# Compressed key scores of a decode step from weighted queries, and unread products in idle stretches

## The chip, the cores and the metric

One core of one Trainium2 chip runs one program, a single launch. The metric is the device time of one execution in microseconds, the median of several runs.

## The reference

One layer of a hybrid decoder is applied to a prompt of 1024 tokens and to 8 decode sequences of 4 new tokens each over a cache of 2048 tokens. All data are fp32. One input projection feeds two head groups: NSA (8 heads in 2 groups, with compressed, selected and window branches) and MLA (4 heads on latent rows). Their outputs are gated, joined, projected, added to the input and normalised.

What matters here is the compressed branch of a decode sequence. A compressed key is formed for every pair of neighbouring 16-token chunks of the cache, and scores are its products with the queries:

```python
def compress(k, w, pe):
    ...
    ch = k[:, :n_chunks * CMP_STRIDE].reshape(B, n_chunks, CMP_STRIDE, G_A, HD_A)
    blk = jnp.concatenate([ch[:, :-1], ch[:, 1:]], axis=2) + pe[None, None, :, None, :]
    return jnp.einsum('bnlgd,lde->bnge', blk, w)

    s = jnp.einsum('btgrd,bngd->btgrn', q, kc).astype(jnp.float32) * scale
```

`w` is 32 token positions by 64 by 64. A sequence has 128 chunks and 127 compressed keys, 2 groups, and 16 query rows (4 tokens by 4 heads) in a group, so 32 rows in all.

## The kernel before

The kernel is written by hand for each engine: the order of the calls is the order in which an engine works, and semaphores with counted values are the only waits. Five stages follow one another: the input projection (0 to 384 us), its preparation and the prompt's attention (to 798), the output projection of 8 prompt tiles (798 to 918), decode of 8 sequences (918 to 1153), and the output projection of the decode rows (to the end).

**Head.** `pe_projection` (L414) multiplies the conditioning rows with w_ada (L427), waits for the sums (`s_us`, `s_modD`), transposes them (L442), waits for the modulation on VectorE (`s_modt`), transposes the first prompt tile's tokens (L554) and starts the decode rows' first projection (L456) when its weights have come.

**Output projection.** In `pe_out` (L1669) a tile m is 8 transposes of the next tile (L1676) and two times 8 calls of 128x128 weights on 512 columns (L1695). In tiles 5 to 7 `chunk` (L1919) adds the first sequence's page transposes between them. VectorE and ScalarE evict and normalise. On SP's queue `sp_out` (L1642) loads what decode needs: biases at m = 1, queries and the compression weights (`load_compressors`, L1969) at m = 2, pages of sequence 0 at m = 3 and 4, its latents and window at 5 and 6.

**Decode.** `pe_decode_loop` (L2060) runs one iteration for each sequence b. TensorE first compresses keys: `compress(b, 0, 0, 16)` is 16 token positions by 2 groups, 32 calls at L2079 with weights of 64 rows by 128 columns (the two halves of the 32 positions side by side) on the 128 chunks. The result stands in banks 3 and 4; ScalarE copies it to RBK with the position bias added (L2259). Window scores (L2090) stand between, then the compressed scores (L2100): 4 calls of a query block `QC`, built by POOL for each sequence, against RBK, shifted by one chunk for the second half. Then come latent scores (L2114), the transposes of the probabilities (L2134 to L2136, which wait on `s_cv` for VectorE's PG, L2366), the value compression (L2079 again, 64 records more), importance, selected scores, the value products (L2153 to L2177), and between them the page transposes of the next sequence (L1925), which VectorE and ScalarE copy to `XT`.

VectorE's order in an iteration: the copy of the former sequence's output (L2341), the turn of the selected keys (L2332), the window scores' subtraction (L2348), the compressed softmax to PG (L2359 to L2366), the copy PTI (L2375), and later the ranking, the other softmaxes, and at the end the turns of window (L2325) and latents (L2309) for the next sequence.

POOL builds `QC`, then the window and selected query blocks `QB` (L2497), then `QM` (L2501); `built(b, n)` is the count that TensorE waits for. Before the first of these it finishes the last tile's norm, which waits for ScalarE's square of that tile (L1760). SP loads 16 pages of 256 KB for a sequence once the buffer is free (L2013), its window (L2024) and 16 latent blocks (L2018). At the end of the last iteration there are no page transposes; TensorE multiplies with FM (L2217, L2224), waits for VectorE's last turn PTS (L2434), forms the selected values (L2175, L2177), two small products (L2231, L2234) and the rows' output projection (L1713), behind which VectorE waits for gate rows loaded in 32 small transfers.

Of the kernel before, what the change touches and what calls it, by code (L numbers as in the profile page):

```python
# [20 lines left out]
P = 128  # L21
# [95 lines left out]
def build(nc, x_prompt, x_sample, cache_nsa, cache_mla, state_win, page_table, c_prompt, c_sample,  # L117
# [3 lines left out]
    with ExitStack() as ctx:  # L121
# [14 lines left out]
        ql_dram = nc.dram_tensor("sample_q_latent", (P, P), F32, kind="Internal").ap()  # L136
        qr_dram = nc.dram_tensor("sample_q_rope", (64, P), F32, kind="Internal").ap()
# [275 lines left out]

        def pe_projection(pe):  # L414
# [5 lines left out]
            for k in range(KT):  # L420
# [10 lines left out]
                if k == 1:  # L431
# [6 lines left out]
                    pe.transpose(PS[:, 0, 128:138], GST[0:10, :], ident[0:10, 0:10]).then_inc(s_u, 1)  # L438
            pe.wait_ge(s_us, 1)
# [3 lines left out]
            mm.then_inc(s_mt, 1)  # L443
            pe.wait_ge(s_modt, 2)
# [1187 lines left out]
        def sp_out_loads(sp):  # L1632
# [7 lines left out]
            sp.dma_start(GF, g_final.rearrange("(o n) -> o n", o=1).to_broadcast([P, DM])).then_inc(s_gp, 16)  # L1640

        def sp_out(sp, tiles, at):  # L1642
            for m, j in enumerate(tiles, at):
# [25 lines left out]
        def pe_out(pe, tiles, at):  # L1669

            def transposes(m, j):
                if m >= 1:
                    pe.wait_ge(s_yTA, m)
                    pe.wait_ge(s_yTD, m)
                for f in range(8):
                    mm = pe.transpose(PS[:, f // 4, P * (f % 4):P * (f % 4) + P], Z[:, j - 1, P * f:P * f + P], ident)  # L1676
# [5 lines left out]
            for m, j in enumerate(tiles, at):  # L1682
# [10 lines left out]
                for c in range(2):  # L1693
# [3 lines left out]
                    mm.then_inc(s_po, 1)  # L1697
                    if m >= 5:
# [48 lines left out]
        def act_out(act, tiles, at):  # L1747
            copy = lambda o, i: act.activation(o, i, ACT.Copy)
            for m, j in enumerate(tiles, at):
# [3 lines left out]
                if m + 1 < at + len(tiles):  # L1753
                    out_copies(act, copy, 0, s_yTA, m + 1)
                if m >= 5:
# [4 lines left out]
                act.activation(JK[0:n, :], YO[m % 2][0:n, :], ACT.Square, accum_out=SSO[0:n, m:m + 1]).then_inc(s_so, 1)  # L1760

# [4 lines left out]
        def dve_out(dve, tiles, at):  # L1766
            for m, j in enumerate(tiles, at):
# [11 lines left out]
                for c in range(2):  # L1779
# [6 lines left out]
                        .then_inc(s_g2, 1)  # L1786
                if m < NT - 1:
# [35 lines left out]
        IMS, IMJ, RK, MK = dsm(30), dsm(15), dsm(15), dsm(16)  # L1823
        G1, G2 = dsm(450), dsm(450)
        DMN, MN, SUM, NMX, RCD = dsm(12), dsm(4), dsm(4), dsm(4), dsm(4)
        QC = [dsm(128).rearrange("p (g s q) -> p g s q", g=G, s=2) for _ in range(2)]
# [10 lines left out]
        WC2 = view(33152, 4096).rearrange("p (k l m) -> p k l m", k=2, l=16)  # L1837
        KT4 = view(42400, 2048).rearrange("p (j c) -> p j c", j=4)
# [24 lines left out]
        RING = [(0, n) for n in CHUNK_ITEMS[0] + CHUNK_ITEMS[1]]  # L1863
# [9 lines left out]
        BY_ACT = {it: it[1] in (("K0", "K2", "K3", "V0", "V2") if it[0] else ("K0", "K2", "V0", "V2")) for it in RING}  # L1873
# [15 lines left out]
        def bank_of(b, name):  # L1889

            m = AT[b, name]
            if m < FRONT:
                return PS[:, 0 if name == "V3" else 6 + m % 2, :]
# [11 lines left out]
        def next_bank(pe, b, name):  # L1905

            m = AT[b, name]
            if m < FRONT:
                if 2 <= m and name != "V3":
# [17 lines left out]


# [22 lines left out]
        def load_queries(sp):  # L1951
# [8 lines left out]
            for s in range(2):  # L1960
                sp.dma_start(QSREP[64 * s:64 * s + 64, :, :, :].rearrange("p g b q -> p g (b q)"),
                             qs_dram.rearrange("(g d) x -> d g x", g=G)).then_inc(s_nb, 16)
            sp.wait_ge(s_qd, 8)
# [5 lines left out]
        def load_compressors(sp):  # L1969
            for k, w in enumerate((w_cmp_k, w_cmp_v)):  # L1970
                for g in range(G):
                    for s in range(2):
                        sp.dma_start(WC2[64 * g:64 * g + 64, k, :, 64 * s:64 * s + 64],
                                     w[0, 16 * s:16 * s + 16].rearrange("l d e -> d l e")).then_inc(s_nb, 16)
# [7 lines left out]
        def load_mask(sp):  # L1982
            sp.wait_ge(s_qd, 9)
# [4 lines left out]
        def load_late(sp):  # L1988
            sp.wait_ge(s_late, 64)
            sp.wait_ge(s_qd, 10)  # L1990
# [9 lines left out]
        NB_EARLY = 16 * (24 + 14 + 3 + 8 + 1)  # L2000
# [26 lines left out]
        def store_window(sp, b):  # L2027
            sp.wait_ge(s_wn[b % 2], 16 * (b // 2) + 16)
# [4 lines left out]
        def sp_decode(sp):  # L2033
            load_mask(sp)
            for b in range(1, NB):
# [8 lines left out]
                load_window(sp, b)  # L2044
                load_latent(sp, b, pages)
# [536 lines left out]
```

## Time and profile before

| | us |
|---|---|
| median of 3 runs | 1170.86 (1169.98 to 1173.89) |
| profiled execution | 1170.58 |
| its span, first to last instruction | 1168.8 |
| TensorE busy (matmul) | 1125.3 |
| VectorE busy | 547.6 |
| ScalarE busy | 350.5 |
| POOL busy | 86.5 |

The mean granted TensorE clock is 0.983 of full speed. The page gives busy time for each engine; an fp32 matmul call appears as two records on TensorE, a transpose as one, and both have a weight load (PEld) each. A mean duration of a record is its latency and is longer than the distance between two, since records overlap: the busy time of a group over its count is the better price. The granted clock is 1.00 at 2.4 GHz and 0.50 at 1.2 GHz.

### The profile page before, as it was taken

To read this page: it belongs to the slowest core of one execution; us is meant where nothing else is said; L and a number is where in the kernel's file an instruction comes from. 1 tells how busy PE (TensorE), PEld (TensorE's weight loads), DVE (VectorE), ACT (ScalarE), POOL (GpSimd) and SP (SyncE) were. 2 spreads that over 40 slices of the span, in tenths; PEclk is the share of its full clock that TensorE was granted. 3 is DMA by queue.
4 is the path that set the end of the run, shared out by engine and by line. 5 is a ranking of instruction groups with operands and counts; after the bars stand their busy time and mean duration, and the time that the engine had idled before them with its cause. 6 is when DMAs were issued, how large, how long until landed. Compare 5 with 4: busy or idle time off the path is not lost.

```text
span 1168.8 us, 21316 instructions
## 1 busy us (share of the span) xinstructions
PE 1125.3 (96%) x7918; PEld 739.6 (63%) x7918; DVE 547.6 (47%) x1486; ACT 350.5 (30%) x839; POOL 86.5 (7%) x209
## 2 busy tenths in 40 slices
PE   6899999899999999999899999999999999999997
PEld 2476767444454567778786676756444677777775
DVE  0211111111111357776767675752333677777773
ACT  0212111101110246555446464641111133322220
POOL 0000000000000011111010000001000200000000
PEclk8899999999999999999999999999999999999997
DMA  9664301200000441000000000002873577676760
GB/s 355 261 211 131 133 28 35 71 4 7 3 4 8 72 90 63 1 2 2 1 1 1 2 1 2 1 1 74 165 284 108 198 243 247 223 249 232 245 189 20
DMA packets 83309, 115.97 MB, mean 99 GB/s; under 512 B 30113, under 2 KB 52052, under 8 KB 82184
## 3 DMA queue, kind: packets, MB, share of 16 engines
q1 hardware_dynamic: 83208, 114.61, 30.9%
q8 instruction: 64, 1.05, 0.4%
q14 instruction: 37, 0.30, 0.1%
HBM read 102.31 MB, written 12.27 MB: 98 GB/s over the span
## 4 chain that ended last, share of the span: by engine, by line
PE 84%; issue 8%; DVE 3%; DMA 2%; ACT 1%; SPq 1%; POOL 0%; ACTq 0%; POOLq 0%; DVEq 0%
PE PS L518 14%; PE PS L1695 9%; PE PS L1390 7%; PE PS L1368 7%; PE PS L1344 6%; PE PS L495 5%; PE PS L463 5%; PE PS L2079 4%; PE PS L1331 3%; PE PS L2114 3%; PE PS L484 3%; PE PS L1365 3%; DMA AR<-in_w_in 2%; PE PS L2127 2%; PE PS L1340 2%
## 5 line engine op out<-in xcount | busy, mean ns | idle before, releaser
L518 PE MATMUL PS<-AR 128*128 128x512 f32 (+1 forms) x384 | 161.3, 580 | 2.7 <-DVE AR L770 2.7
L518 PEld LDWEIGHTS PS<-AR 128*128 128x128 f32 x384 | 72.9, 192 | 86.0 <-issue 82.3
L1390 PE MATMUL PS<-CA,AR 128*128 128x128 f32 x704 | 112.6, 283 | 0.2 <-ACT AR L1444 0.2
L1695 PE MATMUL PS<-AR 128*128 128x512 f32 x256 | 111.7, 592 | 0.0
L1390 PEld LDWEIGHTS PS<-CA,AR 128*128 128x128 f32 x704 | 78.3, 144 | 34.9 <-issue 25.4
L1460 ACT ACTIVATE AR<-PS 128x512 f32<-128x512 f32 (+1 forms) x108 | 58.2, 547 | 138.9 <-PE PS L1390 138.6
L1368 PE MATMUL PS<-AR 128*128 128x65 f32 (+1 forms) x768 | 99.6, 270 | 0.0
L1368 PEld LDWEIGHTS PS<-AR 128*128 128x128 f32 x768 | 94.2, 192 | 0.0
L1444 ACT ACTIVATE AR<-PS,SM_ 128x512 f32<-128x512 f32 (+4 forms) x208 | 83.6, 474 | 17.0 <-DVE SM_ L1525 9.8
L1695 PEld LDWEIGHTS PS<-AR 128*128 128x128 f32 x256 | 47.8, 190 | 56.0 <-issue 56.0
L1344 PE MATMUL PS<-AR 64*128 64x512 f32 (+3 forms) x384 | 74.4, 493 | 6.0 <-ACT AR L1444 4.1
L1492 DVE TENSOR_REDUCE SM_<-PS 128x1 f32<-128x512 f32 (+2 forms) x80 | 41.9, 566 | 61.9 <-PE PS L1340 31.8
L2079 PE MATMUL PS<-AR 64*128 64x128 f32 x1024 | 63.6, 277 | 0.0
L1472 DVE COPY AR<-PS 128x512 f32<-128x512 f32 (+1 forms) x100 | 56.9, 585 | 9.8 <-PE PS L1390 8.9
L2079 PEld LDWEIGHTS PS<-AR 64*128 64x128 f32 x1024 | 59.0, 188 | 2.0 <-issue 1.3
L495 PE MATMUL PS<-AR 128*64 128x128 f32 x1024 | 57.7, 273 | 0.0
L495 PEld LDWEIGHTS PS<-AR 128*64 128x64 f32 x1024 | 55.7, 137 | 2.8 <-issue 2.8
L463 PE MATMUL PS<-AR 128*128 128x512 f32 x128 | 56.3, 593 | 0.7 <-ACT AR L607 0.7
L1441 ACT ACTIVATE AR<-PS,SM_ 128x512 f32<-128x512 f32 (+3 forms) x96 | 54.4, 583 | 2.6 <-DVE SM_ L1525 1.9
L1344 PEld LDWEIGHTS PS<-AR 64*128 64x128 f32 x384 | 31.5, 186 | 30.4 <-ACT AR L1441 11.5
L1525 DVE CUSTOM_DVE_ANT_0 PS<-PS,AR,SM_ 128x256 f32<-128x256 f32 (+1 forms) x96 | 47.3, 535 | 1.7
L1603 POOL TENSOR_TENSOR AR<-AR 128x256 f32<-128x256 f32 x32 | 23.2, 725 | 328.5 <-DVE AR L1591 328.5
(350 smaller groups left out, 1521.3 us busy)
## 6 DMA issues: line engine op xcount, KB each, us to landing
AR<-in_cache_nsa SPq DMA_DIRECT2D x128, 256.0 KB, 4.9
AR<-in_cache_mla SPq DMA_DIRECT2D x128, 96.0 KB, 4.5
AR<-in_x_prompt SPq DMA_DIRECT2D x16, 512.0 KB, 4.6
AR<-in_w_ada SPq DMA_DIRECT2D x3, 2048.0 KB, 11.4
AR<-in_w_in SPq DMA_DIRECT2D x4, 1472.0 KB, 9.6
out<-AR SPq DMA_DIRECT2D x9, 512.0 KB, 3.6
AR<-in_w_ada SPq DMA_DIRECT2D x8, 512.0 KB, 6.1
AR<-in_w_out SPq DMA_DIRECT2D x4, 1024.0 KB, 9.8
```

The costliest lines, as they stand in the source:

```text
L463: mm = pe.matmul(PS[0:n, 3, :], ht(j, k)[:, 0:n], W1[:, k, 512:1024], start=(k == 0), stop=(k == KT - 1))
L495: mm = pe.matmul(PS[64 * g:64 * g + 64, 2, P * r:P * r + n], w1q(k, r, g), ht(j, k)[:, 0:n], start=(k == 0), stop=(k == KT - 1))
L518: mm = pe.matmul(PS[0:n, bank, 0:hi - lo], ht(j, k)[:, 0:n], w2cols(k, lo, hi), start=(k == 0), stop=(k == KT - 1))
L1344: mm = pe.matmul(scores(u, gi, o, o + P * n), QT[rg, r, q], keys[rg, ks], start=True, stop=True)
L1368: mm = pe.matmul(out, tile, v, start=(n == 0), stop=(n == nb - 1))
L1390: mm = pe.transpose(PS[:, 4 + c % 2, P * (t - t0):P * (t - t0) + P], tile(u, t), ident)
L1441: act.activation(probs(u, gi, lo, hi), PSF[:, o + lo:o + hi], ACT.Exp, bias=NM[:, u % 2, gi:gi + 1], scale=-1.0, accum_out=TOT[og % 4][:, ...
L1444: act.activation(probs(u, gi, lo, hi), PSF[:, o + lo:o + hi], ACT.Exp, bias=NM[:, u % 2, gi:gi + 1], scale=-1.0).then_inc(s_exp, 1)
L1460: evac(act, c, lambda o, i: act.activation(o, i, ACT.Copy), s_evA)
L1472: copy(PTB[:, c % 4, 0:nt, :], PS[:, 4 + c % 2, 0:P * nt].rearrange("p (t q) -> p t q", t=nt)).then_inc(done, 1)
L1695: mm = pe.matmul(PS[0:n, 2 + 2 * (m % 2) + c, :], YTO[m % 2][:, f, 0:n], weights[:, f, 512 * c:512 * c + 512], start=(f == 0), stop=(f == 7))
L2079: mm = pe.matmul(PS[:, 3 + g, 0:128], x if k else w, w if k else x, start=(l == 0), stop=(l == 15))
```

## The change

For every key position l the product of query and compression weight does not depend on the cache. It is formed once for all 8 sequences. In tiles 1 to 4 of the output projection `key_turns` transposes four positions of the key weights (behind the first half's calls), ScalarE copies them to `WKT`, and `key_queries` (behind the second half's) multiplies them with the queries, 16 calls of 64x64 weights on 128 columns. VectorE and ScalarE copy one bank each to `QWS`, and SP stores them to DRAM at m = 3 to 6, after the pages and latents. The key weights and the queries are now loaded right before the first tile.

In decode `key_products` replaces the key compression: SP loads 256 KB of weighted queries for each sequence (`load_keyed`, between window and latents, counted on the window's semaphore), and 32 calls with weights of 64 rows by 32 columns on the 128 chunk tokens write to four strips of 32 rows in banks 3 and 4, position l to strip l mod 4. ScalarE copies them to RBK without the bias. `compressed_scores` sums the strips with a constant selection matrix `PICK` (4 calls), after one more call that gives the bias term from the queries `QSB` and `CCB`. POOL's two `QC` products go; one copy `QSB` is made at the start. VectorE's `selected_turn` of sequences 1 to 7 moves from ahead of the window scores' subtraction to behind PG.

`keep_warm` multiplies the identity with constants into a bank that is not read: 1280 columns ahead of L442, 1024 ahead of the wait for the modulation, 768 ahead of the last sequence's selected values. Counts of semaphores follow. The diff, cut to what is spoken of:

```diff
+        def keep_warm(pe, bank, columns):
+            for n in columns:
+                pe.matmul(PS[:, bank, 0:n], ident, CA[:, 0:n], start=True, stop=True)
...
+            keep_warm(pe, 6, (512, 512, 256))
             pe.wait_ge(s_us, 1)
             pe.wait_ge(s_modD, 1)
             for f in range(4):
                 mm = pe.transpose(PS[:, 5, P * f:P * f + P], MODR[:, P * f:P * f + P], ident)
             mm.then_inc(s_mt, 1)
+            keep_warm(pe, 6, (512, 256, 256))
             pe.wait_ge(s_modt, 2)
...
+                if 3 <= m <= 6:
+                    keyed_store(sp, m - 3)
                 if m == 6:
+                    load_keyed(sp, 0)
...
+                    if (m, c) in KEYED:
+                        (key_queries if c else key_turns)(pe, KEYED[m, c])
...
+        KEYED = {(m, c): str(m - 1) for m in range(1, 5) for c in range(2)}
...
+        def key_turns(pe, n):
+            if n == "0":
+                pe.wait_ge(s_scr, 192)
+            pe.wait_ge(s_yTA, int(n) + 3)
+            for l in range(4):
+                mm = pe.transpose(PS[:, 0, P * l:P * l + P], WC2[:, 0, 4 * int(n) + l, :], ident)
+            mm.then_inc(s_it, 1)
+
+        def key_queries(pe, n):
+            wait_read(pe, 0, "T" + n)
...
+            for l in range(4):
+                for g in range(G):
+                    for s in range(2):
+                        rg = slice(64 * s, 64 * s + 64)
+                        mm = pe.matmul(PS[64 * g:64 * g + 64, 7 - s, P * l:P * l + P],
+                                       WKT[rg, P * l + 64 * g:P * l + 64 * g + 64],
+                                       QSREP_FLAT[rg, P * g:P * g + P], start=True, stop=True)
...
+        def keyed_store(sp, n):
...
+            sp.dma_start(qw_dram[:, :, 128 * n:128 * n + 128].rearrange("b p x -> p b x"),
+                         QWS[n].rearrange("p b l s q -> p b (l s q)")).then_inc(s_scr, 16)
...
+        def load_keyed(sp, b):
+            if b == 0:
+                sp.wait_ge(s_scr, 256)
+            if b >= 2:
+                sp.wait_ge(s_r, 2 * (b - 2) + 1)
+            sp.dma_start(QWB[b % 2].rearrange("p l x -> p (l x)"), qw_dram[b]).then_inc(s_wn[b % 2], 16)
...
-            def compress(b, k, lo, hi):
+            def key_products(b):
+                for c in range(4):
+                    wait_read(pe, b, CHUNK_ITEMS[0][c])
+                pe.wait_ge(s_wn[b % 2], 32 * (b // 2) + 32)
+                if b >= 1:
+                    pe.wait_ge(s_cv, 2 * b)
+                else:
+                    pe.wait_ge(s_nb, NB_EARLY)
+                for l in range(16):
+                    for g in range(G):
+                        rg, c = slice(64 * g, 64 * g + 64), RS * (l % 4)
+                        mm = pe.matmul(PS[c:c + RS, 3 + g, 0:128], QWB[b % 2][rg, l, :], XT[rg, 0, l, :],
+                                       start=(l < 4), stop=(l >= 12))
+                mm.then_inc(s_r, 1)
...
             def compressed_scores(b):
                 bank = next_bank(pe, b, "cmp")
+                if b == 0:
+                    pe.wait_ge(s_dv, 2)
+                    pe.wait_ge(s_qd, 9)
+                pe.matmul(bank[0:RS, 0:NCMP_S], QSB[:, b, :, :].rearrange("p g q -> p (g q)"), CCB[:, 0:NCMP_S], start=True, stop=False)
                 pe.wait_ge(s_rk, b + 1)
-                pe.wait_ge(s_qd, built(b, 2))
                 for g in range(G):
                     for s in range(2):
-                        mm = pe.matmul(bank[0:RS, 0:NCMP_S], QC[b % 2][:, g, s, :], RBK[:, g, s:s + NCMP_S],
-                                       start=(g + s == 0), stop=(g + s == 2))
+                        mm = pe.matmul(bank[0:RS, 0:NCMP_S], PICK[:, s, 16 - 16 * g:48 - 16 * g], RBK[:, g, s:s + NCMP_S],
+                                       start=False, stop=(g + s == 2))
...
                 ahead = (lambda name: chunk(pe, b + 1, name)) if b + 1 < NB else (lambda name: None)
-                compress(b, 0, 0, 16)
+                key_products(b)
...
                     pe.matmul(PS[:, 3, 16 * b:16 * b + 16], OMS[:, b, :], FM[:, 0:16], start=True, stop=True)\
                         .then_inc(s_yb2, 1)
+                    keep_warm(pe, 5, (512, 256))
...
-                act.activation(RBK, PS[:, 3:5, 0:128], ACT.Identity, bias=CCON[:, 0:1]).then_inc(s_rk, 1)
+                act.activation(RBK, PS[:, 3:5, 0:128], ACT.Copy).then_inc(s_rk, 1)
...
                     dve.tensor_copy(OYS[:, b - 1, :], O_B[:, 0:128]).then_inc(s_o, 1)
-                    selected_turn(b)
...
                 dve.tensor_scalar(PG[0:RS, 1:128], PC[0:RS, 1:128], GBR[0:RS, b, 0:1], None, ALU.mult)\
                     .then_inc(s_cv, 1)
+                selected_turn(b)
                 if b == 0:
-                    selected_turn(0)
...
+            pool.tensor_copy(QSB.rearrange("p b g q -> p g b q"), QSREP).then_inc(s_qd, 1)
...
-                for g in range(G):
-                    pool.tensor_tensor(QC[b % 2][:, g, :, 16 * g:16 * g + 16],
...
```

## Rows read from the trace of the kernel before

**Rows 1.** The page: busy time and share by engine; chain that ended last.
```profile
PE 1125.3 (96%) x7918; PEld 739.6 (63%) x7918; DVE 547.6 (47%) x1486; ACT 350.5 (30%) x839; POOL 86.5 (7%) x209
PE 84%; issue 8%; DVE 3%; DMA 2%; ACT 1%; SPq 1%; POOL 0%; ACTq 0%; POOLq 0%; DVEq 0%
```

**Rows 2.** Windows of one projection tile and one decode iteration: length, busy by engine, clock, DMA.
```profile
815.50:830.00 14.50, 14.50 (x41) 6.80 (x40) 4.54 (x7) 1.63 (x3) 0.75 (x2) 1.00 0.47 129
1012.00:1043.00 31.00, 30.52 (x309) 22.67 (x309) 24.10 (x53) 8.58 (x15) 1.94 (x5) 1.00 0.74 251
```

**Rows 3.** Groups by shape on TensorE: busy us in all, mean ns of one.
```profile
L2079 PE MATMUL PS<-AR 64*128 64x128 f32 x1024 | 63.6, 277 | 0.0
L2153 PE MATMUL PS<-AR 128*32 128x128 f32 x256 | 8.6, 276 | 0.0
L495 PE MATMUL PS<-AR 128*64 128x128 f32 x1024 | 57.7, 273 | 0.0
```

**Rows 4.** Timeline of one decode iteration: start us, us, engine, line, idle before.
```profile
1035.80 3.84 PE L2079 MATMUL PS<-AR 64*128 64x128 f32 x64
1036.80 3.46 DVE L2309 STREAM_TRANSPOSE AR<-AR 128x1024 f32<-128x1024 f32 x3
1039.57 1.57 PE L2090 MATMUL PS<-AR 128*128 128x192 f32 x8
1040.36 2.29 DVE L2332 STREAM_TRANSPOSE AR<-AR 128x2048 f32<-128x2048 f32 x1
1041.07 0.79 PEld L2100 LDWEIGHTS PS<-AR 128*32 128x32 f32 x8 [0.23 <-issue]
1042.05 3.70 PE L2114 MATMUL PS<-AR 128*128 128x512 f32 x8
1042.58 0.25 DVE L2348 TENSOR_TENSOR AR<-PS,CE 128x128 f32<-128x128 f32 x1
1044.88 0.28 DVE L2366 TENSOR_SCALAR AR<-AR,SM_ 32x127 f32<-32x127 f32 x1
1045.68 0.48 PE L2134 MATMUL PS<-CE,AR 32*128 32x128 f32 x2
```

**Rows 5.** Timeline of TensorE in a projection tile with a chunk's transposes.
```profile
873.94 7.03 PE L1695 MATMUL PS<-AR 128*128 128x512 f32 x16
880.81 0.60 PE L1925 MATMUL PS<-CA,AR 128*128 128x128 f32 x4
881.25 7.03 PE L1695 MATMUL PS<-AR 128*128 128x512 f32 x16
```

**Rows 6.** Timeline at the start of decode, sequence 0.
```profile
922.65 0.76 POOL L2497 TENSOR_TENSOR AR<-AR,CE 128x128 f32<-128x128 f32 x2
923.55 1.54 PE L2090 MATMUL PS<-AR 128*128 128x192 f32 x8
```

**Rows 7.** Timeline of TensorE in the head.
```profile
30.84 1.04 PE L442 MATMUL PS<-CA,AR 128*128 128x128 f32 x4 [2.48 <-ACT AR L587]
37.28 5.89 PE L456 MATMUL PS<-AR 128*32 128x256 f32 x48 [0.96 <-DMA AR<-in_w_in]
```

**Rows 8.** Window of TensorE in the head: busy, clock, DMA share, GB/s.
```profile
41.00:41.50 0.50, 0.50 (x9) 0.80 1.09 422
```

**Rows 9.** Windows of the tail, columns as in rows 2.
```profile
1150.50:1151.00 0.50, 0.00 (x0) 0.00 (x0) 0.50 (x1) 0.00 (x0) 0.00 (x0) 0.53 0.03 10
1157.00:1157.50 0.50, 0.50 (x8) 0.22 (x4) 0.00 (x0) 0.00 (x0) 0.00 (x0) 0.50 0.13 33
1160.50:1161.00 0.50, 0.50 (x12) 0.32 (x8) 0.00 (x0) 0.00 (x0) 0.00 (x0) 0.73 0.00 0
```

**Rows 10.** Timeline of TensorE in the tail.
```profile
1151.48 2.12 PE L2177 MATMUL PS<-AR 128*32 128x128 f32 x29
1155.92 6.03 PE L1713 MATMUL PS<-AR 128*32 128x256 f32 x64
```

**Rows 11.** Timeline of SP's queue in one iteration.
```profile
1016.90 9.47 SPq L2018 DMA_DIRECT2D AR<-in_cache_mla  x16
```

More of the change, by code:

```diff
@@ L1754, in act_out @@
                     out_copies(act, copy, 0, s_yTA, m + 1)
+                if (m, 0) in KEYED:
+                    key_turns_copy(act, copy, KEYED[m, 0])
                 if m >= 5:
@@ L1760, in act_out @@
                 act.activation(JK[0:n, :], YO[m % 2][0:n, :], ACT.Square, accum_out=SSO[0:n, m:m + 1]).then_inc(s_so, 1)
+                if (m, 1) in KEYED:
+                    key_queries_copy(act, copy, KEYED[m, 1], 1, s_rA)
         def out_normed(dve, m):
@@ L1823, in build @@
         IMS, IMJ, RK, MK = dsm(30), dsm(15), dsm(15), dsm(16)
+        WKT = view(dcur[0] + 128, 512)
         G1, G2 = dsm(450), dsm(450)
         DMN, MN, SUM, NMX, RCD = dsm(12), dsm(4), dsm(4), dsm(4), dsm(4)
-        QC = [dsm(128).rearrange("p (g s q) -> p g s q", g=G, s=2) for _ in range(2)]
+        CCB, PICK = dsm(128), dsm(96).rearrange("p (s c) -> p s c", s=2)
         NB15 = dsm(36)
@@ L1837, in build @@
         WC2 = view(33152, 4096).rearrange("p (k l m) -> p k l m", k=2, l=16)
+        QWB = [view(33152 + 512 * n, 512).rearrange("p (l x) -> p l x", l=16) for n in range(2)]
+        QSB = view(34176, 256).rearrange("p (b g q) -> p b g q", b=NB, g=G)
+        QWS = [view(20480 + 1024 * n, 1024).rearrange("p (b l s q) -> p b l s q", b=NB, l=4, s=2) for n in range(4)]
         KT4 = view(42400, 2048).rearrange("p (j c) -> p j c", j=4)
@@ L1862, in build @@
         SMALL_ITEMS = ["cmp", "pts", "fmw", "imp", "smw", "fs", "ss"]
-        RING = [(0, n) for n in CHUNK_ITEMS[0] + CHUNK_ITEMS[1]]
+        KEYED = {(m, c): str(m - 1) for m in range(1, 5) for c in range(2)}
+        RING = [(0, k + str(n)) for n in range(4) for k in "TAB"]
+        RING += [(0, n) for n in CHUNK_ITEMS[0] + CHUNK_ITEMS[1]]
         FRONT = len(RING)
@@ L1872, in build @@
         AT = {it: m for m, it in enumerate(RING)}
[L1873 removed]
+        BY_ACT = {it: it[1] in (("K0", "K2", "K3", "V0", "V2") if it[0] else ("K0", "K2", "V0", "V2", "T0", "T1", "T2", "T3", "B0", "B1", "B2", "B3"))
+                  for it in RING}
         READS = {it: sum(BY_ACT[o] == BY_ACT[it] for o in RING[:m + 1]) for m, it in enumerate(RING)}
@@ L1908, in next_bank @@
             if m < FRONT:
-                if 2 <= m and name != "V3":
+                if name in ("K0", "K1"):
+                    wait_read(pe, 0, "B3" if name == "K0" else "A3")
+                elif name != "V3":
                     wait_read(pe, *RING[m - 2])
@@ L1958, in load_queries @@
                              qr_dram.rearrange("(j c) x -> c j x", c=32)).then_inc(s_nb, 16)
[L1960 to L1963, printed above, removed]
+            sp.wait_ge(s_qd, 6)
             for k in range(2):
@@ L2280, in decode_masks @@
             dve.memset(PG[0:RS, :], 0.0)
+            dve.memset(PICK, 0.0).then_inc(s_dv, 1)
+            dve.wait_ge(s_conv, 2)
+            dve.tensor_copy(CCB, CCON[:, 0:1].to_broadcast([P, 128]))
             dve.wait_ge(s_cst, 80)
+            dve.wait_ge(s_dv, 1)
+            for s in range(2):
+                dve.tensor_copy(PICK[:, s, 16:32], FM[:, 16 * s:16 * s + 16])
             dve.wait_ge(s_nb, NB_EARLY)
@@ L2289, in decode_masks @@
                               .to_broadcast([RS, NB, 4]), ALU.add).then_inc(s_dv, 1)
-            dve.wait_ge(s_dv, 1)
+            dve.wait_ge(s_dv, 2)
         def dve_decode(dve):
-            count = [1]
+            count = [2]
             def step(ins):
@@ L2460, in pool_clear @@
             pool.wait_ge(s_fin, NG)
-            for a in (QB[0], QM[0], QC[0], QC[1]):
+            for a in (QB[0], QM[0]):
                 pool.memset(a, 0.0).then_inc(s_qd, 1)
             pool.memset(GBR[:, :, 3:4], 0.5).then_inc(s_qd, 1)
-            pool.wait_ge(s_qd, 5)
+            pool.wait_ge(s_qd, 3)
             settle(pool)
```

89 lines of the change are left out of this document (57 added, 32 removed).

## Prediction

> **What bounds the kernel now.** I read the page first. TensorE is busy 96% of the span and holds 84% of the chain that ended last [rows 1], so a TensorE microsecond removed is a microsecond gained as long as no other engine becomes late. Then the windows by stage, for how much room the others have: in an output-projection tile TensorE is busy all 14.5 us with VectorE at 4.5 and ScalarE at 1.6, and in a decode iteration it is busy 30.5 of 31.0 us with VectorE at 24.1 [rows 2]. Then the groups by shape, for the price of a record; the timeline of one iteration and of one projection tile, for what starts when; the start of decode, the head and the tail, the three places in which TensorE does idle. The profiled execution took 1170.58 us (span 1168.8 and 1.8 around it); the median shown is 1170.86, so 0.3 is added at the end. An fp32 matmul call leaves two records, a transpose one. All prices are per record.
>
> **Key products (decode).** Before, a sequence's key compression was 32 calls of 64x128 weights against 128 columns: 64 records in 3.84 us [rows 4], 63.6 us over 1024 records, key and value together, so 62 ns, and 60.0 in this stretch [rows 3]. After, the calls number the same and stream the same 128 columns; only the weights are narrower (64x32), in four column strips and two row halves. What is gained is only what eight tiles overlap better than two. The trace has no 64x32 tile. Bounds: 60.0 ns if nothing more overlaps; below, the nearest narrow row, 128x32 in four strips, 8.6 us over 256 = 33.6 ns [rows 3], halved for the two row halves, 16.8. I take 28: nearer to 33.6, as the two halves take turns but each record still has to be issued. Gain: 64 x 32 ns = 2.05 us an iteration (bounds 0 and 2.77).
>
> The Trainium skill (TensorE: Matmul & The Clock Gate, section Back-to-back issue gap) says that matmuls do not start less than about 25 ns apart however small they are. By that figure, an estimate, the gain would be 2.24 us an iteration and the sum some 1.3 us lower. No row here shows that floor; the narrow row above stays over it.
>
> **Compressed scores.** Four calls become five, and all write one strip, so they do not overlap: four calls take 1041.07 to 1042.05, 0.245 each [rows 4]. Plus 0.25 us an iteration. The added call is ahead of the wait for ScalarE's copy, but that copy (0.47 us) lies under the window scores before and after, so no wait is filled by it: the 0.25 is paid.
>
> **Does the rest keep up in an iteration?** If TensorE comes 1.8 us earlier to the transposes of the probabilities (before 1045.68, after 1043.9), VectorE's PG must be there. Before, VectorE ran without a gap: latent turns 1036.80 to 1040.26, the copy, the selected turn to 1042.65, the softmax from 1042.58 with PG ending at 1045.16 [rows 4]. So left as it was, VectorE would have taken 1.3 of the 1.8 us away. The diff moves the selected turn (2.29 us) behind PG. Then the softmax starts at 1040.6 and PG ends 2.57 later, at 1043.2: 0.7 us to spare. The moved turn then stands ahead of the PTI copy and ends at 1045.5; the copy is next needed by the importance product, 4.6 us behind the probabilities in the same timeline, and the selected scores come later still, so it costs nothing. What is late next is PG, if the records went below about 17 ns. POOL no longer builds the two QC blocks: off the path. SP's queue gets one load of 256 KB an iteration, between window and latents; window turns wait for it too. Latent loads are issued until 1026.4 [rows 11], ten us ahead of their turn, and the new load adds 0.5 us of issue and about 0.8 of transfer: nothing. Seven iterations: 7 x (2.05 - 0.25) = 12.6 us.
>
> **Iteration 0 gains nothing.** Its window scores wait for POOL's QB blocks, two of them from 922.65 for 0.76 us, and start 923.55 [rows 6]. That chain comes from ScalarE's square of the last tile and is not shorter (two QC products, 0.44 us, go; a copy of 256 columns comes). TensorE will simply stand idle for 1.8 to 2.1 us ahead of 923.55, and pays 0.25 for the fifth call. Decode in all: -12.4 us (bounds +2.0 and -17.4).
>
> **Output projection.** Four tiles get four transposes and 16 calls of 64x64 weights on 128 columns. TensorE has no gap there, so each is paid in full. Four transposes between projections: 16 records from 873.94 to 880.81, the next 16 at 881.25, so 0.44 us [rows 5]. The calls: 32 records; two-strip 128x64 records cost 57.7/1024 = 56.3 ns, half of it 28.2, four strips 33.6 [rows 3]; I take 32, 1.02 us, bounds 28.2 and 60. Two changes of tile shape, each as ahead of the compressed scores (0.23 [rows 4]) at most: I take 0.35, bounds 0 and 0.46. Sum 1.81 x 4 = +7.2 us (bounds 5.4 and 11.3). The copies (one more on VectorE, two on ScalarE a tile) have ten us of room. The four stores and the first keyed load go through SP behind the pages, all landed a tile or more before the first K chunk is copied.
>
> **Dummy products.** Head: TensorE idles 2.48 us ahead of L442, while the clock is at 2.4 GHz, and falls behind it [rows 7]; the first dummies stream 1280 columns, 2.5 calls of 512, five records of 6.87/16 = 0.429 us [rows 5], 2.15 us, so they fit. The next 1024 columns (1.7 us) fit into the 2.5 us ahead of the token transposes. L456 starts when its weights land, 37.28, whatever the clock; it ran at 1.2 GHz until about 41.2 [rows 8]: 3.9 us at half speed, 1.95 to win. TensorE still idles before 37.28, so the clock may fall anyway: I take 1.0 (0 to 1.95). Tail: the clock fell at about 1150.5 with TensorE idle, and came back at 1160.7 [rows 9]. In between selected values lose 1.1 us, the two small products 1.2, L1713 4.8/2 = 2.4 [rows 10]: 4.7, capped at about 4.5 because the gate-row loads on which the end waits are still moving at 1157.0 to 1157.5 [rows 9], against the end of L1713 at 1161.95. 768 columns are 1.3 us in a gap of 1.54, if at full clock; if it has fallen before them, they take 2.6 and delay the values by 1 us. The products ahead of them are thin, so it may fall first, but come back sooner: I take 2.5 (bounds -4.5 and +1.1).
>
> **Sum.** -12.4 + 7.2 - 1.0 - 2.5 = -8.7: 1161.9 on the profiled time, 1162.2 on the median's level; I say 1162.
>
> **Rivals.**
> (a) The forecast, packing at 25 to 34 ns: 1158 to 1166. 0.58.
> (b) Eight tiles pack fully, 17 ns: decode -17.4, projection +6.8, clock -3.5: 1156.5. For it: each doubling of tiles in [rows 3] nearly halves the record (64x128 62, 128x32 33.6). Against: loads and matmuls of 64 records must be issued. 0.15. The Trainium skill (TensorEngine Tiling (Array Packing), section Available Configurations) lists 64x32 as eight independent tiles, which would be this case.
> (c) Slower: 64x32 and 64x64 run like the 64-row tiles of before, 60 ns, because the two row halves in one strip serialize. Place: key products and key queries. Decode +2.0, projection 4 x (0.44 + 1.92 + 0.35) = +10.8, clock -3.5: 1180. The gain (21.7 us less 0.576 for each ns, before clock effects) is gone at 38 ns, with them at 44. Against it: 64x128 halves do overlap today, and so do strips. 0.09.
> (d) The packing is right but the dummies bring nothing, and the new idle ahead of the window scores of iteration 0 drops the clock for a while (up to 1.5 us): -12.4 + 7.2 + 1.5 = -3.7: 1167. 0.10. The Trainium skill (TensorE: Matmul & The Clock Gate, Part 4: PE-mode transpose) says transposes do not count as activity for the clock; by it the head, where only transposes stand between the dummies and L456, would win nothing. The trace can't tell.
> (e) A new wait eats half: PG or a K chunk copy is late by 1 us an iteration. -12.4 + 7 + 7.2 - 3.5: 1169. The spare 0.7 us speaks against. 0.08.
>
> **Chances.** About 0.3%, 3.5 us, can be told from no change. Faster: (a), (b), and half of (d): 0.78. Same: the rest of (d), (e) less a little: 0.13. Slower: 0.09. The range 1155 to 1170 holds (a), (b), (d) and (e), and leaves out (c).
>
> **What would show it.** The period of an iteration, 29.03 us (the latent scores start at 1013.02 and at 1042.05), down to 27.2; the key products' 64 records in 1.8 us; PG still ahead of the probabilities; idle of 2 us ahead of iteration 0's window scores; tiles 1 to 4 of the projection 1.8 us longer; the clock in the head between 31 and 41 us, and behind 1150. Wrong if a record of 64x32 costs over 40 ns, or TensorE shows idle time in the iterations.

## The result: faster by 1.4%, almost twice the forecast

| | before | after |
|---|---|---|
| median of four runs, us | 1170.51 (1169.98 to 1173.89) | 1155.27 (1154.25 to 1157.75) |
| profiled execution, its span | 1170.58, 1168.8 | 1155.38, 1153.3 |
| mean granted clock | 0.983 | 0.991 |

The ratio is 0.9862, with a 95% interval of 0.9845 to 0.9878. The forecast was 1162, 8.7 us less on the profiled time; measured were 15.2 on it. The direction was right, the size was not. The median lies at the lower edge of the range, and on the level from which the forecast was made, 1170.86, the ratio gives 1154.7, just below it.

The page of the kernel after, the two lines that answer to [rows 1]:
```profile
PE 1110.9 (96%) x8094; PEld 723.2 (63%) x8094; DVE 549.5 (48%) x1494; ACT 353.6 (31%) x847; POOL 83.4 (7%) x192
PE 84%; issue 8%; DVE 3%; DMA 2%; ACT 1%; SPq 1%; POOL 0%; ACTq 0%; POOLq 0%; DVEq 0%
```
The balance is that of before: TensorE holds 96% of the span and 84% of the chain. The kernel became faster by 14.4 us less TensorE time, not by filling idle time, though there are 176 records more. Where the 15.5 us of the span went, by the starts of the same work in both timelines:

| stretch, us | before | after | difference | forecast |
|---|---|---|---|---|
| start to the first output-projection product | 800.89 | 800.77 | -0.12 | -1.0 |
| from there to sequence 0's key products | 118.72 | 125.22 | +6.50 | +7.2 |
| those to sequence 0's window scores | 3.94 | 3.88 | -0.06 | 0 |
| window scores of sequence 0 to those of 7 | 203.00 | 185.22 | -17.78 | -12.4 |
| last window scores to the end | 42.25 | 38.21 | -4.04 | -2.5 |

The -12.4 holds the fifth call of all eight sequences; the eighth of them, 0.25, falls into the last stretch.

**Decode.** Groups by shape on TensorE in the kernel after, columns as in [rows 3]; the first is the value compression, which stayed as it was:
```profile
L2172 PE MATMUL PS<-AR 64*128 64x128 f32 x512 | 32.9, 278 | 0.0
L2161 PE MATMUL PS<-AR 64*32 64x128 f32 x512 | 9.2, 274 | 0.0
L1978 PE MATMUL PS<-SM_,AR 64*64 64x128 f32 x128 | 4.4, 275 | 0.0
```
Busy time over records: 64.3 ns for a 64x128 record, 18.0 for the new 64x32. The "mean ns of one" is of no use here. It is the latency, 274 to 278 ns in every shape, and tiles that overlap share it.

One iteration after the change, the counterpart of [rows 4]:
```profile
1034.61 1.16 PE L2161 MATMUL PS<-AR 64*32 64x128 f32 x64
1035.65 3.46 DVE L2414 STREAM_TRANSPOSE AR<-AR 128x1024 f32<-128x1024 f32 x3
1035.69 1.57 PE L2183 MATMUL PS<-AR 128*128 128x192 f32 x8
1037.19 0.40 PE L2192 MATMUL PS<-AR 128*32 128x127 f32 x2
1037.43 1.03 PE L2196 MATMUL PS<-AR 128*32 128x127 f32 x8
1038.39 3.70 PE L2210 MATMUL PS<-AR 128*128 128x512 f32 x8
1039.21 0.27 DVE L2452 TENSOR_TENSOR AR<-PS,CE 128x128 f32<-128x128 f32 x1
1041.54 0.28 DVE L2470 TENSOR_SCALAR AR<-AR,SM_ 32x127 f32<-32x127 f32 x1
1041.74 2.29 DVE L2437 STREAM_TRANSPOSE AR<-AR 128x2048 f32<-128x2048 f32 x1
1042.03 0.48 PE L2230 MATMUL PS<-CE,AR 32*128 32x128 f32 x2
```
From the first key record to the first window record 1.08 us pass, for 64 records; in [rows 4] it was 3.77. That is -2.69, and 17.0 ns a record (1.08 to 1.09 us in the seven iterations, over 64) where start to start it was 58.9. From the compressed scores to the latent scores 1.20 pass, where it was 0.98: +0.22 for the fifth call. The two make -2.47 of the period's -2.54 (203.00/7 = 29.00 to 185.22/7 = 26.46). And PG now ends at 1041.82, only 0.2 us ahead of the transposes that need it. The selected turn stands behind PG, as the diff puts it.

**The start of decode**, after, answering [rows 6]; the bracket gives the idle time before a row and what ended it:
```profile
925.99 1.16 PE L2161 MATMUL PS<-AR 64*32 64x128 f32 x64
928.97 0.76 POOL L2597 TENSOR_TENSOR AR<-AR,CE 128x128 f32<-128x128 f32 x2
929.87 1.54 PE L2183 MATMUL PS<-AR 128*128 128x192 f32 x8 [2.73 <-POOL AR L2597]
```
What sequence 0's key products save is spent as 2.73 us of waiting for POOL, as forecast (1.8 to 2.1 there, with records of 28 ns).

**The output projection**, a tile with key queries after, answering [rows 5]:
```profile
862.12 1.10 PE L1978 MATMUL PS<-SM_,AR 64*64 64x128 f32 x32
863.15 1.09 PE L1689 MATMUL PS<-CA,AR 128*128 128x128 f32 x8
864.08 7.03 PE L1708 MATMUL PS<-AR 128*128 128x512 f32 x16
870.95 0.60 PE L1966 MATMUL PS<-CA,AR 128*128 128x128 f32 x4
871.39 7.03 PE L1708 MATMUL PS<-AR 128*128 128x512 f32 x16
```
The transposes take 0.44 (870.95 to 871.39) and the key queries 1.03 (862.12 to 863.15), 32 ns a record as forecast. The keyed tiles take 16.24 us (first product to first product, 864.08 to 880.32) against 14.61 (815.50 to 830.11 before), 1.63 more: only 0.16 is left for the shape changes, for which I had added 0.35.

**The head**, TensorE of the kernel after, answering [rows 7]:
```profile
28.34 2.42 PE L417 MATMUL PS<-CA 128*128 128x512 f32 x6
31.44 1.89 PE L417 MATMUL PS<-CA 128*128 128x512 f32 x6
37.37 5.56 PE L463 MATMUL PS<-AR 128*32 128x256 f32 x48 [2.19 <-DMA AR<-in_w_in]
```
And a window right behind, columns as in [rows 8]; behind the busy times of the five engines stand the granted clock, the DMA share and GB/s:
```profile
38.50:39.00 0.50, 0.50 (x7) 0.31 (x3) 0.00 (x0) 0.00 (x0) 0.00 (x0) 0.50 1.05 393
```
In this execution the dummies moved the fall of the clock from 31 us to about 37.2, but did not prevent it: TensorE is idle for 2.19 us ahead of L463, and the first of the projection still runs at 1.2 GHz. That is not the rule. The profile of e6, which has the same dummies here and the same idle time ahead of L463, shows no fall:
```profile
37.14 3.97 PE L463 MATMUL PS<-AR 128*32 128x256 f32 x48 [2.20 <-DMA AR<-in_w_in]
```
Of the ten profiles with head dummies seven (e1, e2, e5, e6, e8, e9, e12) keep 2.4 GHz from 26 us on to past this projection, which then takes 3.97 us; three (the kernel after, e7, e11) fall at it, and it takes 5.56 to 5.66. The four without them (before, e10, e3, e4) all fall between 30 and 33 us, and it takes 5.89 to 6.64.

**The tail**, TensorE of the kernel after, answering [rows 10], and a window of it, answering [rows 9]:
```profile
1138.33 1.54 PE L417 MATMUL PS<-CA 128*128 128x512 f32 x4
1140.16 1.14 PE L2273 MATMUL PS<-AR 128*32 128x128 f32 x29
1142.78 3.66 PE L1728 MATMUL PS<-AR 128*32 128x256 f32 x64 [0.25 <-DVE AR L2551]
```
```profile
1142.00:1146.00 4.00, 3.75 (x65) 2.80 (x68) 1.09 (x4) 0.00 (x0) 0.00 (x0) 1.00 0.07 21
```
The clock stays at 2.4 GHz until these products are done. The selected values take 1.14 us instead of 2.12, and the output's last products 3.66 instead of 6.03.

### The profile page after: what moved, and what is told of

Its sections match the earlier page's. It is cut to its first block, busy times and chain, and to the rows that moved or that the text cites. A ratio compares the mean times of both kernels' runs of the same rounds, so it can differ in the third digit from the quotient of the medians.

```text
span 1153.3 us, 21698 instructions
## 1 busy us (share of the span) xinstructions
PE 1110.9 (96%) x8094; PEld 723.2 (63%) x8094; DVE 549.5 (48%) x1494; ACT 353.6 (31%) x847; POOL 83.4 (7%) x192
## 4 chain that ended last, share of the span: by engine, by line
PE 84%; issue 8%; DVE 3%; DMA 2%; ACT 1%; SPq 1%; POOL 0%; ACTq 0%; POOLq 0%; DVEq 0%
PE PS L525 14%; PE PS L1708 10%; PE PS L1397 7%; PE PS L1375 7%; PE PS L1351 6%; PE PS L502 5%; PE PS L470 5%; PE PS L1338 3%; PE PS L2210 3%; PE PS L491 3%; PE PS L1372 3%; DMA AR<-in_w_in 2%; PE PS L2172 2%; PE PS L2223 2%; PE PS L1347 2%
## 5 line engine op out<-in xcount | busy, mean ns | idle before, releaser
L1708 PE MATMUL PS<-AR 128*128 128x512 f32 x256 | 112.3, 592 | 0.0
L470 PE MATMUL PS<-AR 128*128 128x512 f32 x128 | 56.3, 593 | 0.7 <-ACT AR L614 0.7
L1351 PEld LDWEIGHTS PS<-AR 64*128 64x128 f32 x384 | 31.7, 186 | 30.5 <-ACT AR L1448 11.5
L2210 PE MATMUL PS<-AR 128*128 128x512 f32 x96 | 45.2, 608 | 0.0
L1801 DVE TENSOR_TENSOR AR<-PS,AR 128x512 f32<-128x512 f32 x16 | 11.1, 692 | 71.1 <-PE PS L1708 71.1
```

Of the source, the lines that this page charges most:

```text
L470: mm = pe.matmul(PS[0:n, 3, :], ht(j, k)[:, 0:n], W1[:, k, 512:1024], start=(k == 0), stop=(k == KT - 1))
L1351: mm = pe.matmul(scores(u, gi, o, o + P * n), QT[rg, r, q], keys[rg, ks], start=True, stop=True)
L1708: mm = pe.matmul(PS[0:n, 2 + 2 * (m % 2) + c, :], YTO[m % 2][:, f, 0:n], weights[:, f, 512 * c:512 * c + 512], start=(f == 0), stop=(f == 7))
L2210: pe.matmul(S_B, QM[b % 2][:, j, :, :].rearrange("p i q -> p (i q)"), MLT[j // 2][:, j % 2, :], start=(j == 0), stop=(j == 5))
```

## The experiments

The theory after the result: the extra gain is the price of a 64x32 record, some 17 ns where 28 was taken, because column strips and row halves overlap independently; the dummies (the products that `keep_warm` adds) give what was forecast. Its rivals: the extra is chance in the clock, which another set of runs would take away; or the gain comes from another edit (the moved turn, or dummies worth more than 3.5 us). Each experiment edits the kernel after, unless it says otherwise.

**e1: the two row halves one after the other.**
```diff
-for l in range(16):
-    for g in range(G):
+for g in range(G):
+    for l in range(16):
```


> The changed kernel with the key products' two row halves one behind the other (all 16 positions of group 0, then of group 1) in place of alternating. Theory: the 17 to 18 ns of a 64x32 record come from eight tiles, four strips times two halves; with one half at a time only four strips overlap and a record costs about 33.6 ns as the 128x32 records of before do, so the 64 records take 2.15 in place of 1.09 us, seven iterations +7.4 us, the first sequence nothing (it has 2.7 us of idle): about 1162.5 us. Rival: 64x32 records are cheap because of their small weight loads alone, and the order of the halves doesn't matter: 1155.


Measured: 1159.8, ratio 0.9907 (0.988 to 0.9933). The period is 26.87, 0.41 more. TensorE in that iteration:
```profile
1034.40 1.56 PE L2161 MATMUL PS<-AR 64*32 64x128 f32 x64
1035.90 1.57 PE L2183 MATMUL PS<-AR 128*128 128x192 f32 x8
```
1.50/64 = 23.4 ns a record. So the row halves do overlap, and taking them in turn is worth 6.4 ns a record; but even four strips of one half cost less than the 28 ns that 128x32 records take start to start (below); why is not shown. The expected 33.6 was wrong by the same fault as the forecast. The rival, that the order of the halves doesn't matter, is refuted.

**e7: the key products twice.** It gives the marginal price of 64 records.
```diff
+for again in range(2):
     (the loop over l and g, indented)
```


> The changed kernel with the 32 calls of the key products done twice over (same result). Theory: 64 records more at 17 ns are 1.09 us an iteration in seven of them, and nothing in the first, where they fill the idle time ahead of the window scores: +7.6 us, 1162.9. Rival: at the 28 ns of the prediction +12.5 us.


Measured: 1163.52, 0.9924 (0.9903 to 0.9944); the period is 27.34, 0.88 more. TensorE:
```profile
1039.57 2.03 PE L2162 MATMUL PS<-AR 64*32 64x128 f32 x128
1041.53 1.57 PE L2184 MATMUL PS<-AR 128*128 128x192 f32 x8
```
The second 64 records cost 0.88/64 = 13.75 ns each, below the 16.8 that was my bound. The first 64 cost 0.2 us more than the second; that this is a start-up is an interpretation.

**e9: the same strip four times running.**
```diff
-for l in range(16):
+for l in [4 * i + j for j in range(4) for i in range(4)]:
```


> The changed kernel with the key products' positions in an order in which all four that write one strip follow one another (strip 0, then 1, 2, 3); the two row halves still alternate. Theory: eight tiles overlap because consecutive records are in other strips; here only the two halves can, as in the 64x128 records of before, so a record costs about 53 ns, the 64 records 3.4 in place of 1.1 us, seven iterations +16 us: 1171. Rival: narrow weights alone make the record cheap: 1155.


Measured: 1166.64, 0.9946 (0.9925 to 0.9967); the period is 27.80, 1.34 more. TensorE:
```profile
1037.34 2.48 PE L2161 MATMUL PS<-AR 64*32 64x128 f32 x64
1039.76 1.57 PE L2183 MATMUL PS<-AR 128*128 128x192 f32 x8
```
2.42/64 = 37.8 ns: records for a tile that is addressed again soon do cost more, though less than the 53 expected. In the changed kernel the same tile comes up again after eight calls, in e1 after four, in e9 after two; the same 64 records then cost 17.0, 23.4 and 37.8 ns. Half of what was saved against 58.9 hangs on the order of the calls, the other half comes with the narrow shape even in the bad order. Each tile always writes the same strip of the same bank, so no run tells whether the wait is for the part of the array or for the sums that it writes.

**e5: the changed kernel again, unedited.**


> The changed kernel as it is, once more. The clock fell near 432 us, in a stretch that no edit touches, in the kernels without the head's dummies, and cost some 5 us there; theory A: whether it falls there follows from how long the head takes, so this one repeats 1155 with no fall near 432. Theory B: it is chance of the execution, and some runs here show 1160.


Measured: 1155.64, 0.9861 (0.984 to 0.9881); in the first set of runs it was 0.9862. So the gain is not chance of one set of runs. But one of the five runs took 1162.2, and it is the profiled one. A window of it, then the same window of e6, in which only the tail's dummies are left out:
```profile
434.00:440.00 6.00, 6.00 (x30) 5.32 (x30) 2.88 (x15) 2.53 (x9) 0.00 (x0) 0.50 1.01 330
```
```profile
434.00:440.00 6.00, 5.25 (x47) 4.77 (x44) 4.66 (x20) 4.34 (x18) 0.72 (x1) 1.00 1.00 353
```
In e5 TensorE works for 6 us at 1.2 GHz, and gets through 30 records where e6 has 47. Some 2 us ahead of the fall TensorE was idle for 1.2 us, until 428.89, waiting for ScalarE; e6 has the same wait, until 428.27, and no fall. The output projection starts at 802.98 in e5 and at 798.96 in e6; 0.62 of these 4.02 us arise in the head (42.38 against 41.76 for the first prompt projection), 3.4 behind it. So theory B holds, chance of the execution: e5 is the kernel whose first profile had no fall there.

**e3: no dummies; e4: only the tail's; e6: only the head's.**
```diff
-keep_warm(pe, 6, (512, 512, 256))      # e3, e4
-keep_warm(pe, 6, (512, 256, 256))      # e3, e4
-keep_warm(pe, 5, (512, 256))           # e3, e6
```


> The changed kernel without any unread products. Theory: the tail runs at 1.2 GHz for some 10 us as before (end of the last sequence's values to the end of the rows' projection 4.3 us longer), the head changes by 0.1 to 0.3: about 1159.5 us. Rival: the tail's clock is set by the moment at which the end comes, not by the dummies, and would have stayed up anyway: 1155.

> The changed kernel with the 768 unread columns of the tail only. Theory: the head's two groups of dummies bring 0.1 to 0.3 us, since the clock falls in the idle time ahead of the first decode projection either way: 1155.5 us, and the tail stays at full clock. Rival: the head's dummies are worth 1 to 2 us: 1157.

> The changed kernel without the 768 unread columns of the tail, with the head's. Theory A: no fall near 432, and the tail about 4.5 us longer than with them: 1159.7. Theory B (the tail's columns bring at most 1 us, the rest was the moment): 1156.


Measured: e3 1165.62, 0.9948 (0.993 to 0.9966); e4 1162.91, 0.9926 (0.9909 to 0.9943); e6 1158.7, 0.9893 (0.9872 to 0.9914). e6 lost 3.1 us against e5, which ran beside it, close to the 2.5 forecast. e3 and e4 lost 6 and 7 us more than expected. Their profiles show falls near 432 (both), 933 (e3) and 568 (e4). The tail of e3, to be held against that of the kernel after:
```profile
1145.38 2.12 PE L2271 MATMUL PS<-AR 128*32 128x128 f32 x29
1149.82 6.22 PE L1726 MATMUL PS<-AR 128*32 128x256 f32 x64
```
These are the slow durations of [rows 10] again. From the last window scores to the end the four profiles without tail dummies (before, e10, e3, e6) take 42.25, 42.27, 43.55 and 42.71, mean 42.70; nine with them take 38.14 to 41.28, mean 39.98. That is 2.7 us, where 2.5 was forecast. The tenth, e2, takes 43.26: it has that run's added wait and fall (below) in this stretch too, and with it the difference is 2.4. Like with like it is 3.0 both for the kernel before (42.26 against e11's 39.28) and for the changed one. The pair of the result showed 4.0 because in the kernel after the clock did not fall ahead of the last products; besides it, that holds for e7 alone. In the other eight it falls ahead of the dummies or among them, but comes back before the last products, which so take 3.66 us in all ten and 6.03 to 6.27 in the four without dummies. In e5:
```profile
1142.80 2.91 PE L417 MATMUL PS<-CA 128*128 128x512 f32 x4
1149.57 3.66 PE L1728 MATMUL PS<-AR 128*32 128x256 f32 x64 [0.25 <-DVE AR L2551]
```
In the same way the first prompt projection starts at 44.43 on average without head dummies (four profiles) and at 42.84 with them (ten): 1.6 us, where 1.0 was forecast and the pair showed 0.24. In e3's and e4's profiles the rest lies in falls elsewhere: from the first prompt projection to the output projection they lose 1.4 and 3.6 us against the kernel after, and in sequence 0 e3 loses 1.6 more. Such falls also strike the unedited kernel, in e5.

**e11: the kernel before, with the three dummies.**
```diff
+keep_warm(pe, 6, (512, 512, 256))
+keep_warm(pe, 6, (512, 256, 256))
+keep_warm(pe, 5, (512, 256))
```


> The kernel before with only the unread products, at the same three places. Theory: the dummies are worth the same without the rest: head about 1.7 us (first projection of prompt tokens starts that much earlier), tail 3 us (last window scores to the end), together 1166. Rival: they gain only where the changed kernel shifts the moments: 1170.


Measured: 1168.21, 0.9964 (0.995 to 0.9978), -4.2 us. With the head and tail above (1.6 + 2.7 = 4.3) it agrees on average; e11's own profile is one of the three whose clock falls at L463, and gains next to nothing in the head and 3.0 in the tail. So in the kernel before the dummies are worth 4.2 us and, if they are worth as much in the changed one, the rest of the change is 0.9862/0.9964 = 0.9898, about 12 us; the stage table has -17.78 + 6.50 = -11.3. Taken from the other side, e3 to the kernel after, the dummies would seem to be worth 10 us. The two profiles are 9.6 apart: 5.3 in the tail and 1.2 in the head, and 3.0 in e3's falls near 432 and 933. Its profile is one, but five of its six runs took 1165 and more; why is open.

**e2: the selected turn back to its old place. e10: the same move made in the kernel before.**
```diff
 (e2, behind the OYS copy)
+selected_turn(b)        # b >= 1
 (e2, behind PG)
-selected_turn(b)
+selected_turn(0)        # b == 0 only
```


> The changed kernel with the turn of the selected keys back ahead of the window scores' subtraction in sequences 1 to 7. Theory: VectorE's PG is then ready only 2.3 us later, TensorE (which now comes 2.56 us earlier, and had 0.5 us to spare before) waits for it about 2.0 us an iteration ahead of the probabilities, so 14 us of the gain go: about 1169 us. Rival: the probabilities' products are not where the turn matters, since other work stands behind; 1155 to 1157.

> The kernel before with only the turn of the selected keys moved behind PG. Theory: nothing, since before PG is ready 0.5 us ahead of the products that need it; the move is worth its 2 us an iteration only once TensorE comes earlier: 1170.5. Rival: it is a gain by itself of up to 0.5 us an iteration: 1167.


Measured: e10 1172.87, 1.0005 (0.9993 to 1.0017): alone the move brings nothing. e2 1191.26, 1.018 (1.0159 to 1.0201): 36 us worse than the kernel after and 21 worse than before. An iteration of e2, VectorE and TensorE, and a window behind it:
```profile
1081.88 2.30 DVE L2437 STREAM_TRANSPOSE AR<-AR 128x2048 f32<-128x2048 f32 x1
1086.42 0.27 DVE L2471 TENSOR_SCALAR AR<-AR,SM_ 32x127 f32<-32x127 f32 x1
1086.84 0.45 PE L2230 MATMUL PS<-CE,AR 32*128 32x128 f32 x2 [2.06 <-DVE AR L2471]
```
```profile
1088.00:1092.00 4.00, 4.00 (x20) 2.29 (x20) 0.51 (x1) 0.00 (x0) 0.00 (x0) 0.57 1.05 396
```
The turn delays PG, and TensorE waits 2.06 us for it. That alone is the expected 2.0 an iteration (28.55 in those at full clock, +2.09). But of the six full iterations with such a wait only two stay at full clock. In the other four the clock falls behind the wait, and they take 30.1 (two) and 33.3 (two). Against the 26.46 of the changed kernel a wait of 2.06 us so costs 3.6 and 6.8 where the clock falls behind it. Those falls make most of the difference between the 14 us expected and the 36 measured. The turn's move is worth nothing alone, and the gain in the iterations depends on it. That the move was the gain's source is refuted by e10; what the forecast said of it held.

**e8: sequence 0's QB and QM blocks built a tile earlier** (cut; the semaphore counts follow).
```diff
 (pool_out, at m == NT - 2)
+pool.wait_ge(s_nb, NB_EARLY)
+pool.wait_ge(s_cst, 80)
+query_blocks(pool, 0)
 (act_out, last tile, ahead of the wait for s_g2)
+read_chunk(act, copy, 0, "V2")
```


> The changed kernel with POOL's QB and QM blocks of sequence 0 built in tile 6 of the projection and ScalarE's copy of V2 ahead of the last square. Theory: the first window scores start about 2.0 us earlier behind the key products (2.7 us of idle become 0.7, set by VectorE's window turn), the probabilities of sequence 0 follow, so 1.5 to 2.0 us less: 1153.5. Rival: VectorE, with the V3 copy and the last norm in its way, holds back PG of sequence 0 and nothing is gained.


Measured: 1155.91, 0.9863 (0.9843 to 0.9883), the same as e5 beside it. TensorE and VectorE in e8:
```profile
925.66 1.16 PE L2166 MATMUL PS<-AR 64*32 64x128 f32 x64
927.49 1.54 PE L2188 MATMUL PS<-AR 128*128 128x192 f32 x8 [0.68 <-issue]
938.35 0.23 DVE L2423 TENSOR_SCALAR AR<-CE,AR 128x4 f32<-128x4 f32 x1
938.63 0.39 PE L2246 MATMUL PS<-AR,CE 128*128 128x8 f32 x2 [0.45 <-DVE AR L2423]
```
The wait for POOL is gone: key products to window scores take 1.83 us, not 3.88, so 2.05 were won. But 0.49 of it is given back in the same iteration, where VectorE, with the selected turn ahead of the spread L2423, now comes late. The net to sequence 1's window scores is 30.30 to 28.74, -1.56 us; the median does not show it, and the scatter of the clock's falls (1154.05 to 1162.2 in e5) is wider.

**e12: e8, and one dummy at the start of the attention**, in the gap near 430.
```diff
+keep_warm(pe, 7, (512,))
```


> The kernel of e8 (blocks of sequence 0 built early) with 512 unread columns more in the 1.2 us gap at the start of the prompt's attention, near 429 us, behind which the clock fell in half of the profiles and cost about 4 us. Theory: no fall at 432, so the median goes to 1153 to 1154 and the runs over 1158 are gone. Rival: the fall comes from thin work there, not from the gap, and remains: 1155.5.


Measured: 1153.69 (1152.75 to 1155.33, five runs), 0.9845 (0.9829 to 0.9862). The dummy:
```profile
427.54 1.10 PE L417 MATMUL PS<-CA 128*128 128x512 f32 x2
```
It fits into the idle time, and its profile has no fall at 432; nor have eight of the 13 profiles without it, so one profile can't show an effect, and the expectation's rival, thin work, stays open. This is the lowest median of all, and no run of it is over 1156, where the changed kernel has three of nine over it. Against that kernel's ratio the intervals overlap, so only the gain over before is shown.

## Why the prediction missed the size

**The step that failed is the price of the 64x32 record: "I take 28".** The mechanism was right, this term of the sum was mis-sized: measured are 17.0 ns in place and 13.75 for the next 64. The span became 15.5 us shorter and the forecast was 8.7; decode holds 5.4 of the 6.8 missed. Start to start the key products gained 2.69 us an iteration and not 2.05, 7 x 0.64 = 4.5; the fifth call, at 0.22, gives 0.2, and the rest, 0.7, is 0.2 from the call that belongs to the last stretch and 0.5 in small differences over seven iterations (2.54 a period, of which 2.47 are traced). Outside decode the missed 1.4 us are 0.7 in the projection and 1.5 in the tail, less 0.9 in the head. Two faults made the 28.
- The 33.6 was busy time over records of a group with only 32 records at a time. Each such burst ends with its last record's latency, of which 0.18 us lie here under the next work. The price on TensorE's path is start to start, and what I wrote with the profile before, that busy time over count is the better price, holds only for long bursts. In the kernel before:
```profile
1028.54 1.08 PE L2153 MATMUL PS<-AR 128*32 128x128 f32 x32
1029.44 0.27 PE L2157 MATMUL PS<-AR 128*32 128x128 f32 x1
```
  0.90/32 = 28 ns, not 33.6. Halved, that is 14: the marginal price that e7 found. The row was there to be read.
- I did not give the row halves their factor of two, on the ground that "each record still has to be issued". No row spoke for such a floor; the lower bound of 16.8 came from rows, and 28 was a wish to stay in between. e1 and e9 show what the row halves and the strips give in the alternating order, and what it costs without.

**The other steps**
- *Compressed scores* +0.25: measured +0.22. Right.
- *Does the rest keep up:* right, and closer than foreseen. The spare time of PG was to be 0.7 us and is 0.2, since the records came to 17 ns, the very point at which I had put its end. e2 shows what that spare time is worth.
- *Iteration 0 gains nothing:* right (-0.06).
- *Output projection* +7.2: measured +6.5. Transposes and key queries were right to 0.02; the shape changes were taken at 0.35 a tile and 0.16 is left for them.
- *Head* -1.0: the pair shows -0.24 at the first prompt projection, ten profiles against four -1.6. The 1.95 to win is right where the clock holds (5.89 in before, 3.97 in seven profiles of ten), and the doubt, that it may fall in the idle time anyway, is right in three. In rival (d) the head was to win nothing if transposes don't count for the clock; it won, though whether they count can't be told, since the dummies ahead of them may be what holds it.
- *Tail* -2.5: measured -4.0 in the pair, -2.7 over 13 profiles (-2.4 with e2). Right, also in that the clock mostly falls before the dummies and comes back sooner; the size of the pair was luck.
- *Rival (b)*, 1156.5, was the case that came: decode -17.4 (measured -17.8), projection +6.8 (+6.5), clock -3.5 (-4.2). It had 0.15 and should have had most of (a)'s chance. *(c)* fell: no serialization at 60 ns, except that e9 shows 38 when strips repeat. *(d)* and *(e)* did not occur in the pair, though (d)'s mechanism, a fall behind the wait of sequence 0, is real: in the profiles of e2, e3 and e5 the clock is low from 933 or a little before, and sequence 0 takes 28.00, 28.04 and 27.99 us instead of 26.42. That is 1.6, close to (d)'s 1.5.

## What to carry to other kernels

Price a record by start to start of a whole burst, not by busy time over count of short groups. In this kernel a split along both columns and rows paid on both, when the calls went round all tiles before one came up again (17, 23 and 38 ns with eight, four and two tiles in turn). When TensorE becomes faster in a loop, move the next-latest VectorE work before it matters: its move was worth nothing in the kernel before, and its lack cost 36 us after. One profiled pair can't size an edit that acts on the clock: here the pair showed 0.24 and 4.0 where 14 profiles show 1.6 and 2.7, and adding the dummies to the kernel before gave 4.2 us where leaving them out of the changed one cost 10.

## What was not expected of the hardware

**Eight small tiles overlap.** 64x32 tiles run at 17.0 ns a record in place and 13.75 at the margin, against 58.9 for 64x128, start to start. The Trainium skill (TensorEngine Tiling (Array Packing), Available Configurations) lists 64x32 as eight independent tiles, and the runs agree. The Trainium skill (TensorE: Matmul & The Clock Gate, Back-to-back issue gap) puts matmuls at least about 25 ns apart. Counted by records the runs contradict that, with 17.0 and 13.75; counted by fp32 calls of two records, 34 and 27.5, they lie just over it. No run here tells which of the two the sentence means.

**Short waits can cost the clock, or not.** A window in the kernel before:
```profile
434.00:440.00 6.00, 5.25 (x47) 4.73 (x45) 5.09 (x24) 4.18 (x15) 0.00 (x0) 1.00 1.03 287
```
Near 430 TensorE waits 1.2 us for ScalarE in all kernels but e12, which has its dummy there. In this one and in eight others the clock stays at 2.4 GHz behind it; in five profiles of 14 (e2, e3, e4, e5, e7) it is at 1.2 GHz for some 10 us. Nine profiles take 757.0 to 757.2 us from the first prompt projection to the output projection. All nine have two shorter falls in this stretch, near 218 and near 563. Of the five, e4 and e5 have one of these two and take 760.8 and 760.6; e2, e3 and e7 have neither and take 758.5 to 758.6. So an execution with the fall near 432 loses 1.4 to 3.7 us net, and the falls of one execution hang together. The same kernel so runs anywhere from 1154.05 to 1162.2. What decides it in an execution stays open. A dummy of 512 columns in the gap was free; that it prevents the fall is not shown by the one profile with it.
